# The mLSTM's silus and first two stacks at the mLSTM's own beginning, two of its four output-gate products in front of its first unit

## The reference

```python
u = causal_depthwise_conv(concat(q, k))        # 4 taps
q, k = split(silu(u))                          # 4 heads of 64 each, 2 x 256 columns
...
D = where(causal, b[:, None] - b[None, :] + i[None, :], NEG_INF)
w = exp(D - m[:, None])
s = einsum('td,sd->ts', q, k * 64 ** -0.5) * w
num = s @ v                                    # and the sum of s for the divisor
...
out = sigmoid(o_gate) * head_norm(num / max(|sum|, exp(-m)))
```

## Time and profile before

| | us |
|---|---|
| median of three runs | 1764.94 (1763.94 to 1767.94) |
| the profiled execution, whole | 1766.69 |
| its span in the trace | 1764.7 |
| PE busy | 1718.1 (97%) |
| DVE busy | 869.4 (49%) |
| ACT busy | 612.1 (35%) |
| NSA ends and the mLSTM begins on PE | at 1137.61 |
| first matmul behind the mLSTM's last E | at 1189.65 |

### The profile page before, as it was taken

The page is one execution under the profiler, slowest core; times in us unless marked ns, Lnnn a source line. Parts: engine busy times, 40 slices in busy tenths (PEclk is TensorE's granted clock), DMA queues, the critical chain, the costliest instruction groups (busy, mean ns, idle before and its releaser), DMA issues.

```text
span 1764.7 us, 24709 instructions
## 1 busy us (share of the span) xinstructions
PE 1718.1 (97%) x10330; PEld 1301.7 (74%) x10330; DVE 869.4 (49%) x1682; ACT 612.1 (35%) x1077; POOL 129.2 (7%) x82
## 2 busy tenths in 40 slices
PE   8999999999999999999999999999999999999998
PEld 7878867888655555555578967777888888888786
DVE  4455553554465555755553576645734632222223
ACT  4433365423111111111152456653535522222222
POOL 1000110321000000000000000010101100001121
PEclk9999999999999999999999999999999999999999
DMA  8512210468999999999946312125411232213201
GB/s 301 175 48 72 83 50 25 167 269 334 416 423 424 423 424 424 423 425 425 416 159 227 118 51 72 29 66 203 144 48 60 73 131 95 96 48 143 95 25 48
DMA packets 84131, 338.75 MB, mean 192 GB/s; under 512 B 6531, under 2 KB 16387, under 8 KB 67120
## 3 DMA queue, kind: packets, MB, share of 16 engines
q1 hardware_dynamic: 80384, 330.31, 48.0%
q0 software_dynamic: 2336, 4.20, 0.7%
q10 hardware_dynamic: 1296, 2.62, 0.4%
HBM read 329.75 MB, written 10.51 MB: 193 GB/s over the span
## 4 chain that ended last, share of the span: by engine, by line
PE 85%; DMA 6%; DVE 5%; ACT 2%; issue 1%; POOL 0%; SPq 0%; DVEq 0%; POOLq 0%; ACTq 0%
PE ps L577 80%; DMA otf<-in_w 5%; PE ps L3167 1%; PE ps L1027 1%; DVE splitr L652 1%; PE ps L859 1%; PE ps L2268 1%; PE ps L2313 1%; DMA hd<-xf 1%; DVE xf L3572 1%; DMA arenaf<-in_w_out 0%; ACT splitr L663 0%; DVE arenaf L3251 0%; DVE arenaf L3264 0%; ACT arenaf L1016 0%
## 5 line engine op out<-in xcount | busy, mean ns | idle before, releaser
L577 PE MATMUL ps<-hr,splitr 128*128 128x512 f32 (+1 forms) x2784 | 571.0, 364 | 2.2 <-DVE hr L913 1.1
L577 PEld LDWEIGHTS ps<-hr,splitr 128*128 128x128 f32 x2784 | 470.1, 190 | 83.4 <-issue 4.5
L577 PE MATMUL ps<-splitr,hr 128*128 128x512 f32 (+1 forms) x1488 | 274.5, 343 | 1.4 <-DVE hr L1129 0.8
L577 PEld LDWEIGHTS ps<-splitr,hr 128*128 128x128 f32 x1488 | 234.3, 190 | 34.8 <-issue 2.0
L652 DVE TENSOR_TENSOR splitr<-ring,splitr 128x2048 fp32r<-128x2048 f32 x60 | 141.5, 2360 | 204.6 <-ACT splitr L663 204.5
L2385 DVE TENSOR_TENSOR xf<-xf,ps 128x512 f32<-128x512 f32 x248 | 153.3, 680 | 55.7 <-PE ps L577 55.6
L577 PE MATMUL ps<-arenaf 128*64 128x256 f32 (+7 forms) x1376 | 173.2, 363 | 4.2 <-DMA arenaf<-in_w 1.8
L663 ACT CAST splitr<-ring 128x2048 fp32r<-128x2048 f32 x60 | 114.1, 1904 | 135.0 <-PE ps L577 135.0
L2339 ACT ACTIVATE junkr<-ps,arenaf 64x512 fp32r<-64x512 f32 x62 | 42.3, 682 | 293.6 <-PE ps L577 292.8
L577 PEld LDWEIGHTS ps<-arenaf 128*64 128x64 f32 (+2 forms) x1376 | 106.5, 151 | 44.5 <-issue 13.6
L652 DVE TENSOR_TENSOR splitr<-arenaf,splitr 128x2048 fp32r<-128x2048 f32 x27 | 62.4, 2309 | 101.4 <-ACT splitr L663 101.4
(11 more groups left out here) (442 smaller groups left out, 1904.9 us busy)
## 6 DMA issues: line engine op xcount, KB each, us to landing
ring<-in_w SPq DMA_DIRECT2D x22, 2048.0 KB, 24.7
arenaf<-in_w SPq DMA_DIRECT2D x22, 2048.0 KB, 23.6
splitf<-in_w SPq DMA_DIRECT2D x20, 2048.0 KB, 24.7
hf<-in_w SPq DMA_DIRECT2D x20, 2048.0 KB, 25.1
otf<-in_w SPq DMA_DIRECT2D x11, 2048.0 KB, 24.6
ring<-in_w_in SPq DMA_DIRECT2D x10, 2048.0 KB, 9.3
ring<-in_w_gate_up SPq DMA_DIRECT2D x7, 2048.0 KB, 7.9
arenaf<-in_w_in SPq DMA_DIRECT2D x4, 2048.0 KB, 9.1
```

The lines of the kernel that those rows point to most:

```text
L577: return te.matmul(out, lhsT, rhs, start=start, stop=stop)
```

## The change

Three things are moved; nothing is added or taken away in arithmetic.

1. The four silus leave `se_values` in NSA and go to the beginning of `se_ml`, behind ACT's wait for NSA's end.
2. The stack of head 0 leaves NSA (ACT after step 28, DVE after step 29) and the stack of head 1 leaves step 0 of the mLSTM; both go behind the silus on ACT and to the beginning of `ve_ml` on DVE. SP's code is as before; its stack DMAs wait for the new places.
3. On PE the first four of the eight beats of `og` (the groups 0 and 1, which need piece 0 alone) are issued in front of A(0). The other four are shared out over 13 steps by `share(4, 13, u)`: they fall on the steps 3, 6, 9 and 12. ACT and DVE keep their beats at the old steps, `ml_beats`.

```diff
--- before.py
+++ after.py
@@ -3055,9 +3055,6 @@
                     *se_done("gates", ("qk", c)))
 
             def se_values(c):
-                if c == 1:
-                    for n in range(4):
-                        se_conv_gate(n)
                 se_keep("mv", by_columns(mv))(c)
 
             def ve_conv(c):
@@ -3085,6 +3082,8 @@
 
             def se_stack(h):
                 mine, _, k, q = stack_rows(h)
+                for w in se_at(("qk", h // 2), ("qk", 2 + h // 2)):
+                    se.wait_ge(*w)
                 se.copy(STACK[h][0][mine, :], k)
                 se.copy(STACK[h][1][mine, :], q).then_inc(*se_done("stacks high", ("stack high", h)))
 
@@ -3234,8 +3233,6 @@
                 for part, u in nsa_steps(("B", "N", "beat", "E")):
                     if part == "beat":
                         go(beats, nsa_beats(u))
-                        if u == 29:
-                            ve_stack(0)
                         continue
                     p, i, br = NSA[u]
                     cell, sc = NCELL[u % 5], nsa_scores(u)
@@ -3279,8 +3276,6 @@
                 for part, u in nsa_steps(("C", "B", "beat", "E")):
                     if part == "beat":
                         go(beats, nsa_beats(u))
-                        if u == 28:
-                            se_stack(0)
                         continue
                     p, i, br = NSA[u]
                     cell, sc = NCELL[u % 5], nsa_scores(u)
@@ -3342,7 +3337,7 @@
                        12: [("table", 1), ("split", 0)], 13: [("spread", 1), ("split", 1)],
                        14: [("times", 1), ("square", 2), ("split", 2)], 15: [("mean", 2), ("split", 3)],
                        16: [("table", 2)], 17: [("spread", 2)]}
-            ML_STACKS = {0: 1, 3: 2, 7: 3}
+            ML_STACKS = {3: 2, 7: 3}
 
             def ml_beats(s):
                 return share(8, 13, s)
@@ -3355,9 +3350,10 @@
                 beats = beats_F("og", H2, 8, banks=BESIDE)
                 for w in pe_at(*kept("mv", 8)):
                     te.wait_ge(*w)
+                go(beats, 4)
                 for part, u in steps(16, 1, 2):
                     if part == "beat":
-                        go(beats, ml_beats(u))
+                        go(beats, share(4, 13, u))
                         for what, k in ML_SIDE.get(u, []):
                             pe_head(k, "m", what)
                         continue
@@ -3414,6 +3410,12 @@
                 beats = beside(se_lead, ("og", se_ogate, 4, 2))
                 for w in se_at(*S.ends("nsa")):
                     se.wait_ge(*w)
+
+                for h in range(2):
+                    se_conv_gate(h)
+                    se_conv_gate(2 + h)
+                for h in range(2):
+                    se_stack(h)
 
                 def powers(u):
                     h, j = ML[u]
@@ -3489,6 +3491,8 @@
                 beats = beside(ve_lead, ("og", lambda c: None, 4, 2))
                 for w in ve_at(*S.ends("nsa"), ("mcol1",)):
                     ve.wait_ge(*w)
+                for h in range(2):
+                    ve_stack(h)
                 for part, u in steps(16, 1, 2):
                     if part == "beat":
                         go(beats, ml_beats(u) + (u == 13))
```

## The result

| | before | changed |
|---|---|---|
| median of the runs beside each other, 6 each, us | 1764.44 | 1774.28 |
| lowest to highest, us | 1762.22 to 1768.2 | 1771.69 to 1778.26 |
| the profiled execution's own time, us | 1766.69 | 1771.69 |
| its span, us | 1764.7 | 1769.7 |
| its mean granted clock | 0.996 | 0.996 |

The ratio is 1.0054 [1.004, 1.0068]: the change makes the kernel slower by 0.54%, some 9.5 us. Run once more it gave 1772.51 us and 1.0041 [1.0026, 1.0056], some 7 us. (The ratios are those of the record; they are not quotients of the medians.) The direction was forecast; the size was not: +4.3 us was said, and 1774.28 us lies above the range that ends at 1773.0.

A forecast was written before the change was run, and what follows sets the result against it. PE was taken as the bound, busy 1718.1 of 1764.7 us. The terms -1.17 + 0.4 + 2.8 + 1.2 + 1.1 = +4.3 us gave 1764.94 + 4.3 = 1769.2 us, slower by 0.25%, range 1766.0 to 1773.0.

The forecast's parts named there:

- stack 0 out of NSA: NSA, DVE copy freeing the output's bank: PE's idle time falls from 1.33 to 0.16 us, a gain of 1.17 us.
- silus out of NSA: NSA, ACT's table loads and four activations: moving them gains 0, with 0.24 us as upper bound.
- wait at A(0): First unit's A part in the mLSTM: silus, stack 0 and its DMAs finish before 1147.48, so no wait, 0.
- wait at E(0), step 2: mLSTM step 2: with no beat between A(0) and E(0), PE waits for the weighting, 0.4 us.
- wait at step 3: mLSTM step 3: PE's beat waits for DVE's low part of piece 1, made behind weighting 3; 2.8 us.
- wait at step 9: mLSTM step 9: the beat opening group 3 waits for ACT's copy of group 1 out of its bank; 1.2 us.
- wait at the mean of head 1: mLSTM step 11: its beat gone, the mean comes up early and waits for the square; 1.1 us.
- the low clock: Rival: stretches at 1.2 GHz at steps 2 and 3, and 7 and 8, add +2 to +3 us: 1771.5 us; chance 0.20.
- the likeliest case: The forecast itself: four mLSTM waits less NSA's stack gain, +4.3 us, own range 1768.0 to 1770.5; chance 0.47.
- the cover of the front: Start of the mLSTM: four beats, 11.04 us, hide silus, table loads, stacks and DMAs, landing at 1146.0 before 1147.48.
- A(0) late: Rival, front of the mLSTM: stack 0's DMAs land late and A(0) waits 0.8 us: 1770.0 us; chance 0.08.

The follow-up runs named there:

- experiment 6: The kernel before, with only DVE's share of head 0's stack moved two steps later in NSA (step 31, not 29): 1765.77 us, 0.9994.
- kernel 3: The kernel before, with only PE's og beats in the new order, silus and stacks left where they were: 1776.61 us, 1.0059.
- 1: The changed kernel, with ACT and DVE splitting piece 1 of og in the front, ahead of the first unit: 1770.82 us, 1.0023.
- 2: The changed kernel, plus 16 matmuls into unread columns on PE in front of step 3's beat: 1772.38 us, 1.0037.
- 5: The changed kernel, with the four later og beats on PE at steps 6, 8, 11, 12 instead of 3, 6, 9, 12: 1766.31 us, 1.0008.
- 7: The changed kernel, with ACT's and DVE's beats moved as PE's, four in front, others at steps 3, 6, 9, 12: 1775.32 us, 1.0041.
- 8: As kernel 7, but the four later beats at steps 3, 8, 11, 12 on all three engines: 1771.33 us, 1.0027.
- 9: Kernel 7, plus six matmuls into unread columns at each of steps 4, 5, 7 and 8: 1778.57 us, 1.0071.
- 1 again: Kernel 1 run once more unchanged, with a second profile: 1769.69 us, 1.0027.
- 7 again: Kernel 7 run once more unchanged, with a second profile: 1772.88 us, 1.0044.
- kernel 4: The changed kernel, with PE's og beats back at their old steps, so only silus and stacks are moved: 1773.28 us, 1.0047.

## Why the prediction was right and wrong

| step of the prediction | said | idle time in the row | from start to start, less before |
|---|---|---|---|
| stack 0 out of NSA | -1.17 | 1.33 to 0.16 us: -1.17, also alone (experiment 6) | -1.17 |
| silus out of NSA | 0 | not seen as a gain | 0 |
| wait at A(0) | 0 | 0 | 0 |
| wait at E(0), step 2 | 0.4 | 0.29 | 0.41 |
| wait at step 3 | 2.8 | 3.17, with line 652 as the releaser | 3.34 |
| wait at step 9 | 1.2 | 1.04, for ACT's copy | 1.21 |
| wait at the mean of head 1 | 1.1 | 1.11 | 1.27 |
| sum of these | +4.3 | +4.4 | +5.1 |
| the low clock | none in the likeliest case | a stretch of some 7 us at step 3; the mean clock over the runs 0.0022 lower | 2.5 + 0.4 |

The forecast counted on PE from start to start, so the last column is the one to hold against it. The idle time in a row is smaller because it begins where the busy length of the matmul ahead ends, and before, without a wait, that length reached 0.16 to 0.17 us beyond the next start at these four places (before step 3's beat, 1143.34 + 0.28 against 1143.45).

**Right.** The bound, and that nothing was to be won but the stack; the cover of the front, whose nearest rival (A(0) late) did not come; every wait by its place and to 0.5 us, and its releaser but for the mean of head 1. Both table loads cost what their rows say. In the changed kernel the load starts at 1134.20, and the first silu 1.30 us later; the load back to exp:

```profile
1140.27 1.28 ACT L3427 ACT_TABLE_LOAD   x1
1141.57 0.62 ACT L3427 ACTIVATE arenaf<-arenaf,mcol 128x384 f32<-128x384 f32 x1
```

Again 1.30 us from start to start. The drain that the Trainium skill ("ScalarE: Activation LUTs", section "What ACT_TABLE_LOAD costs") adds, with which each switch would take 2.66 us, is not seen here either. What the forecast said the drain would do to its sum, about 0.5 us more, does not follow from its own rows: ACT's high part of piece 1 would be ready at 1150.6 + 2.8 = 1153.4, and DVE asks for it at 1151.5, so it would have been 1.9 us.

**Wrong: the low clock was made a rival of 0.20 and given nothing in the sum.** The prediction's own words named the place ("at the steps 2 and 3 (with the 2.8 us wait)") and its price, +2 to +3 us. It then set it aside because the clock had fallen "once in this stage" before. That was no evidence on the changed stage: before, there was no wait of 3 us in it. The forecast had itself read that the clock had fallen on bare steps without a long wait, so steps that are both bare and waiting were a likelier place than any that the trace of before held. What the runs showed in its place: the clock falls in the wait at step 3, the twelve matmuls behind it take 5.26 us where 2.76 had been counted, and the E behind them 0.3 to 0.4 us more, some 2.8 us in all, in both profiles of the changed kernel and in kernel 3. The waits by themselves, 4.4 us, would have given 1764.44 + 4.4 = 1768.8 us, which is the forecast. The mean clock of the runs, 0.9960 to 0.9938, is 0.0022 x 1770 = 3.9 us of (1 - clock) x span, by the slope 3.0 us. That makes 1771.8; the rival's 1771.5 was near it.

**Too small: the wait at step 3.** Said was 2.8 us, and from start to start it costs 3.34. Of the 0.54 us, 0.49 are the low part itself, which the forecast took at 2.29 us and which takes 2.78 in the changed kernel, beside an addition on POOL. POOL stood in no term of the sum.

**What stays open.** At equal clock the two kernels differ by 5.2 to 5.6 us. The waits from start to start make 5.1, and step 9's beat and the mean of head 1 take 0.2 us more than before. The same count, without what the low clock adds, can be made for every kernel:

| kernel | waits and work from start to start, less before | at equal clock |
|---|---|---|
| changed | +5.2 | +5.6, +5.2 |
| 1 | +2.3 | +2.8, +2.5 |
| 2 | +5.2 | +4.6 |
| 3 | +6.1 | +7.0 |
| 5 | +0.3 | +0.2 |
| 7 | +1.9 | +1.9, +2.8 |
| 8 | +1.0 | +1.6 |
| 9 | +7.2 | +7.8 |

The two agree to 1 us, which is what the numbers are good for, and 0.9 us in kernels 3 and 7 is the most that is left over. Between the two runs of the changed kernel lies their mean clock, 0.9938 and 0.9947, 1.2 us by the slope: the repeat, at 1772.51, lies within the range that had been given, so how far the first median stands above it is in part chance. And what exactly lets the clock fall is not settled. Shown is: with the long wait at step 3 the stretch begins in it (three profiles: the changed kernel twice, kernel 3), without it not there (kernels 1, 1 again, 2, 5, 7, 7 again, 8, 9); in kernel 4 it begins in the wait of 9.45 us. But other stretches come on bare steps, kernels 7 and 8 pay as much for those with hardly a wait, and in kernels 1 and 2 one appears further on that neither profile of the changed kernel had. Whether a stretch at step 3 and one at step 11 stand for each other was not shown.

## What to carry to other kernels

Where products of a second job are laid between dependent steps as filler, each piece of it also covers a wait, and moving it costs what it covered: write for every one down what would wait if it were gone, and for every one that comes earlier, which other engine must have made its operand by then. Here four beats in front were free, and the places of the other four made nearly the whole loss. And where a change puts a wait of some 3 us into a part that was bare of long matmuls already, count the matmuls behind it at half clock in the likeliest case, not as a rival: in all three profiles with such a wait here they ran so.
